# The per-head score loop of a hybrid decoder step: sample memories at steps 1 to 16 instead of 2 to 17

## The reference

```python
def step(carry, inp):
    C, n, m = carry
    qc, kc, vc, ic, fc = inp
    b = jnp.cumsum(fc, axis=-1)
    d = jnp.where(causal, b[..., :, None] - b[..., None, :] + ic[..., None, :], -jnp.inf)
    inter = b + m[..., None]
    m_t = jnp.maximum(inter, jnp.max(d, axis=-1))
    s = jnp.einsum('bhtd,bhsd->bhts', qc, kc) * jnp.exp(d - m_t[..., None])
    a = jnp.exp(inter - m_t)
    num = a[..., None] * jnp.einsum('bhtd,bhdv->bhtv', qc, C) + jnp.einsum('bhts,bhsv->bhtv', s, vc)
    den = a * jnp.einsum('bhtd,bhd->bht', qc, n) + jnp.sum(s, axis=-1)
    h = num / jnp.maximum(jnp.abs(den), jnp.exp(-m_t))[..., None]
    ...
    C_new = decay[..., None, None] * C + jnp.einsum('bhsd,bhsv->bhdv', wk, vc)
```

## Time and profile before

| | |
|---|---|
| median of 3 runs | 3322.55 us |
| the profiled execution | 3323.48 us, of which its span is 3321.7 us |
| PE busy in the span | 95% |
| DVE, ACT, POOL busy | 43%, 24%, 24% |
| score loops: length, from the first product behind the prompt's memory to END's numerators | head 0 104.8, head 1 102.9, head 2 103.5, head 3 103.5 us |

### The profile page before, as it was taken

One profiled execution on the slowest core, in us unless ns is written; L12 is line 12 of the kernel. 1 busy time (PEld: TensorE's weight loads), 2 busy tenths in 40 slices (PEclk: granted clock), 3 DMA queues, 4 the chain that ended last, 5 costly groups with the idle time before them and its releaser, 6 DMA issues.

```text
span 3321.7 us, 51916 instructions
## 1 busy us (share of the span) xinstructions
PE 3161.0 (95%) x20960; PEld 2913.0 (88%) x20960; DVE 1437.7 (43%) x2086; ACT 810.3 (24%) x1525; POOL 813.4 (24%) x519
## 2 busy tenths in 40 slices
PE   6999899999999999999888999899899999999997
PEld 5777599999999989999767877777898999999996
DVE  2000435333333354343338595858425433333335
ACT  4111524111111124111234344343104211111113
POOL 2111033333223232333101010101332333333320
PEclk9999899999999999999889999999899999999998
DMA  7544311111111113333335554636511111111111
GB/s 213 136 119 112 97 39 51 51 44 44 38 51 50 38 45 125 113 111 109 121 129 184 176 199 161 214 120 235 203 41 38 51 51 44 48 47 44 44 38 53
DMA packets 275649, 318.07 MB, mean 96 GB/s; under 512 B 23565, under 2 KB 215309, under 8 KB 274298
## 3 DMA queue, kind: packets, MB, share of 16 engines
q1 hardware_dynamic: 255265, 250.27, 24.6%
q10 hardware_dynamic: 12960, 40.04, 3.1%
q0 software_dynamic: 7296, 25.96, 2.3%
HBM read 224.88 MB, written 92.19 MB: 95 GB/s over the span
## 4 chain that ended last, share of the span: by engine, by line
PE 80%; DVE 9%; ACT 5%; issue 3%; DMA 2%; SPq 0%; DVEq 0%; ACTq 0%
PE ps L366 22%; PE ps L367 22%; PE ps L368 22%; PE ps L1852 3%; PE ps L1046 1%; DMA CT<-in_state_mlstm_C 1%; PE ps L1026 1%; ACT X L449 1%; PE ps L1055 1%; DVE CT L1388 1%; PE ps L1056 1%; PE ps L1057 1%; DVE DN L1498 1%; PE ps L387 1%; PE ps L743 1%
## 5 line engine op out<-in xcount | busy, mean ns | idle before, releaser
L366 PE MATMUL ps<-AH,WH 128*128 128x352 f32 x3072 | 1000.7, 326 | 11.2 <-DVE AL L2298 6.2
L367 PE MATMUL ps<-AL,WH 128*128 128x352 f32 x3072 | 986.3, 321 | 0.0
L368 PE MATMUL ps<-AH,WL 128*128 128x352 f32 x3072 | 986.2, 321 | 0.0
L353 POOL TENSOR_SCALAR WH<-RAW 128x1024 fp32r<-128x1024 f32 x200 | 234.6, 1173 | 1734.3 <-PEq L373 1661.8
L366 PEld LDWEIGHTS ps<-AH,WH 128*128 128x128 f32 x3072 | 577.7, 188 | 37.7 <-issue 23.5
L367 PEld LDWEIGHTS ps<-AL,WH 128*128 128x128 f32 x3072 | 579.1, 189 | 1.0
L368 PEld LDWEIGHTS ps<-AH,WL 128*128 128x128 f32 x3072 | 577.4, 188 | 0.0
L355 POOL TENSOR_TENSOR WL<-RAW,WH 128x1024 fp32r<-128x1024 f32 x200 | 507.7, 2538 | 16.7
L366 PE MATMUL ps<-HH,WH 128*128 128x352 f32 x1536 | 498.4, 324 | 0.0
L367 PE MATMUL ps<-HL,WH 128*128 128x352 f32 x1536 | 492.3, 320 | 0.0
L368 PE MATMUL ps<-HH,WL 128*128 128x352 f32 x1536 | 491.9, 320 | 0.0
(11 more groups left out here) (287 smaller groups left out, 3482.8 us busy)
## 6 DMA issues: line engine op xcount, KB each, us to landing
RAW<-in_ffn_w SPq DMA_DIRECT2D x128, 512.0 KB, 3.8
CT<-in_state_mlstm_C SPq DMA_DIRECT2D x32, 1024.0 KB, 8.6
out_C_s<-CT SPq DMA_DIRECT2D x32, 1024.0 KB, 5.5
RAW<-in_ml_w_in SPq DMA_DIRECT2D x32, 512.0 KB, 3.9
RAW<-in_conv_w_pw SPq DMA_DIRECT2D x24, 512.0 KB, 7.5
STK<-u_scratch SPq DMA_DIRECT2D x48, 190.0 KB, 3.5
xc_scratch<-XC ACTq DMA_DIRECT2D x16, 528.0 KB, 2.7
so_scratch<-SO ACTq DMA_DIRECT2D x16, 528.0 KB, 3.7
```

Source lines behind the costliest of these rows:

```text
L353: pool.tensor_scalar(WH[:, k % 4], RAW[:, k % 2], 1.0, 0.0, ALU.mult, ALU.add).then_inc(w_hi, 1)
L366: pe.matmul(ps[:, bank, 0:CW], wh[:, k, cols], hi[:, k, cs], start=(k == 0), stop=False)
L367: pe.matmul(ps[:, bank, 0:CW], wh[:, k, cols], lo[:, k, cs], start=False, stop=False)
L368: mm = pe.matmul(ps[:, bank, 0:CW], wl[:, k, cols], hi[:, k, cs], start=False, stop=(k == nk - 1))
```

## The change

Two numbers change. SLOT0 becomes 1 and LAST[DEC] becomes 16:

```diff
         DEC, END = 3, 4
-        LAST = {0: 1, 1: 5, 2: 11, DEC: 17, END: 19}
-        SLOT0 = 2
+        LAST = {0: 1, 1: 5, 2: 11, DEC: 16, END: 19}
+        SLOT0 = 1
         IS_STEP = SLOT0 + 2 * DEC_B - 2
```

## The result

The changed kernel takes 3327.39 us (median of 12 runs, 3324.85 to 3331.53), the kernel before on the same chip 3321.33 us (12 runs, 3318.05 to 3323.64): +6.1 us, ratio 1.002, 95% interval 1.0013 to 1.0028. The forecast was 3331 us, 8 us above the kernel before. Slower is the right direction, and 3327.39 lies in the forecast's own range, at its lower end, somewhat nearer to rival B's 3325 than to 3331. The change is 0.18%: by the 0.2% that the prediction asked of a measurable change it would still count as none, while the interval leaves out 1.

The account below looks back on a forecast made before the run. Bound: load 7's release, its length, then PE's work to the denominators. Per head -3.45 + 2.0 + 0.6 + 3.4 = +2.55 us, head 0 +0.65; +8.3 on 3322.55 gives 3331 us, own range 3327 to 3335.

Parts of the forecast that it names:

- rival B: No measurable change, 3325 us: clock stays up at sample 5's read, slow stretch behind sums costs no more; chance 0.24.
- term 1: Sample 5's last update on DVE moves from step 13 to 12, releasing load 7 sooner: -3.45 us a head.
- term 2: DVE is later from step 1 on, by late scores of pair 3 and a second update: +2.0 us a head.
- term 3: Sample 5's read, step 11: its load wait may lower the clock and delay pair 13's scores: +0.6 us (0 to 1.2).
- the load itself: Load 7, of the last sample memory, keeps its length of 9.28 us: 0.
- term 4: One more step of prompt work on PE between load 7's landing and the denominators, partly at low clock: +3.4 us.
- its own sign: In the profile after, the prediction counts as wrong if load 7's wait is gone; 1 to 2.3 us was expected.
- Rival A: The clock falls at load 7's read as well, some 2.1 us per head: 3339 us; chance 0.20.
- Term 5: ACT's copy of the old sums gives DVE pair 18's weights 0.5 us later, hidden by a cover of 4.6 us.
- Head 0: Special case: the wait for load 4 goes, worth -1.9 us, so its loop changes by +0.65 us.

Follow-up runs that it names:

- e9: e6 with DVE's six copies and splits of the tokens moved ahead of its first weighting: 3325.3 us.
- e11: e5 with DVE's six copies and splits of the tokens moved ahead of its first weighting: 3319.9 us.
- e8: The changed kernel with five filler matmuls (results unused) on PE ahead of sample 5's read: 3324.8 us.
- e1: The kernel before, with SP issuing the load of sample b+2 ahead of its wait for sample b's last update: 3326.4 us.
- e2: The changed kernel, with SP issuing the load of sample b+2 ahead of its wait for sample b's last update: 3325.6 us.
- e10: e6 with the sample sums and the denominators' place put back by one step: 3320.8 us.
- e12: e6 with both edits, token splits first as in e9 and sample sums one step later as in e10: 3322.3 us.
- e6: e2 plus filler matmuls (6 and 6, results unused) ahead of PE's two long waits for numerators: 3324.5 us.
- e5: e1 plus filler matmuls (5 and 6, results unused) ahead of PE's two long waits for numerators: 3317.0 us.
- e7: The kernel before with five filler matmuls (results unused) on PE ahead of sample 5's read: 3316.7 us.

## Why the prediction was right, and where not

Head by head the sum can be followed with the measured terms, all counted from the loop's start, as differences to the kernel before. The first three rows give the fourth, by how much load 7 is issued later; the fourth to the seventh give the last:

| | predicted | head 1 | head 2 | head 3 |
|---|---|---|---|---|
| term 1, one step sooner | -3.45 | -3.45 | -3.45 | -3.45 |
| term 2, start (delay at pair 12) | +2.0 | +2.15 | +2.14 | +2.14 |
| term 3, load 5 (further delay at pair 13) | +0.6 | +1.57 | +3.64 | +0.22 |
| load 7's issue, as measured | -0.85 | +0.29 | +2.34 | -1.08 |
| from there to sample 7's read ("the load itself") | 0 | -1.64 | -1.59 | -1.62 |
| term 4, from the read to the denominators | +3.4 | +3.67 | +4.55 | +3.34 |
| from the denominators to END's numerators | 0 | -0.08 | -0.47 | +0.90 |
| loop | +2.55 | +2.24 | +4.83 | +1.54 |

The first three rows add up to the fourth within 0.02 us in every head. Term 1 is the old spacing, kept as it was predicted.

**Term 2 was right in size**: +2.15 for +2.0, and 1.41 for the 1.35 that the scores of pair 3 come later. Its reason was half right. The wait for the mask is there (1.21 us; 1.5 predicted), but e9 and e11 show the same 1.4 us without it: the read and the quarter ahead of the scores are enough.

**Term 3 is the step that was mis-sized**: 0.2 to 3.6 us, mean 1.8 over three heads, where 0.6 with ends of 0 and 1.2 stood. The waits of 1.70 and 2.12 us that it took as a guide were for load 4; those for load 5 were 0, 2.01, 1.25 and 1.85 us in heads 0 to 3. Two more numbers were missing. The load takes 10.5 to 10.8 us instead of 9.6 to 9.8, perhaps since its issue moved closer to POOL's two transfers of 512 KB. And the low clock, when it comes, can take the whole of the scores (3.62 us). e8 takes the wait away and gives heads 1 and 2 back 1.4 and 3.4 us.

**The load itself was put at 0 and gave 1.6 us a head.** The prediction kept load 7 at 9.28 us. In heads 1 to 3 it takes 7.1 to 7.4 us, and PE reaches the read 7.68 us behind the issue instead of 9.3. No reason for the shorter load was found. With it the bound that the forecast named, landing of load 7 plus PE's work, is gone: PE's read comes 0.2 to 0.6 us behind the landing. The prediction had called itself wrong if load 7's wait was gone, and in three of four heads it is; by its own sign its mechanism failed there. Load 7 is not far from binding, though: e8 waits for it in every head. e1 and e2 show that the wait is not what keeps the loops long either: without any wait for loads they stay at 104.7 to 105.8 us. Rival A, the clock falling at load 7's read too, so had no place to happen; its mechanism was real, but at load 5.

**Term 4 was near**: +3.7, +4.6 and +3.3 for +3.4. The order costs, as e10 and e12 show (3.7 and 3.0 us over four heads). The share of the clock in it was too small: the scores of pair 19 took 1.96 us at the low clock, 0.9 more than at the full one, where 0.4 was put for the whole slow stretch.

**A wait that the prediction does not have** stands behind the denominators in head 3, 1.47 us for the store of tile 2. It is there in head 3 of every kernel with the samples at slot 1 except e9 (0.24 to 2.12 us), and in none with them at slot 2.

**Term 5**: not quite hidden. DVE gets the weights of pair 18 some 0.5 us later, as predicted (it waits 2.25 for 1.77 us), but in heads 1 to 3 PE waits 0.35 us for ACT's copy of the old sums, to which ACT comes only behind the gain (until 1988.55 in the chain). The prediction looked at DVE's wait there and not at PE's.

**Head 0**: the wait for load 4 is gone, as predicted, which is worth 1.5 us by pair 12 where 1.9 was put. Sample 5's read waits 2.01 us and the clock stays up, so term 3 is nothing there; from the read of sample 7 to the denominators it is +2.5 instead of +3.4. The loop is 0.5 us shorter where +0.65 stood.

So the total of +8.1 for +8.3 in the loops is right partly by luck. In heads 1 to 3 term 3 was too small by 1.2 us on average and term 4 by 0.45, and the 1.6 us by which PE's read follows sooner on load 7's issue made up for them. The measured time is also 2 us under the loops' sum, by differences outside them that nobody predicted. The direction was not luck: the start (2 us a head at pair 12) and the end's order each cost, as e6, e10 and e5 show with the loads out of the way.

## What to carry to other kernels

When two engines take turns as the bound, taking a wait away moves the idle time instead of removing it; look where it gathers, because one piece of idle on PE can bring the low clock and cost more than several short ones. Where an idle piece can't go, a few matmuls in it may pay: 11 in each head made e1 into e5, 9 us faster. Look at more than one pass of a loop before naming the cause, too: e7 was faster in heads where its reason did not apply. And before moving work one step sooner, write down what each of its transfers will then run beside, and what stands behind it on the engine that is slowest at that moment.

## What the runs showed of the hardware

The length of a wait does not by itself tell whether the clock falls. In the kernel before, 2.01 us at sample 5's read in head 1 were followed by a clock of 0.50. In the changed kernel the same 2.01 us in head 0 were not, nor were 2.74 us in head 2 of e2. Timeline of PE and the window behind it:

```profile
1795.71 1.06 PE L1114 MATMUL ps<-CT,QZ 128*32 128x512 f32 x8 [2.01 <-DMA CT<-in_state_mlstm_C]
```
```profile
1797.00:1799.00 2.00, 2.00 (x11) 1.71 (x10) 1.97 (x4) 0.00 (x0) 0.36 (x1) 1.00 1.01 291
```

Loops with the same instructions in one execution so differ by 3.2 us (head 2 against heads 1 and 3), and single heads shouldn't be compared without looking at their clock.

The clock also falls with PE recorded as busy: in e10 the windows at the sample sums show PE busy for all of their 2.00 us when it goes from 1.00 to 0.50, and in e6 the only wait near is one of 0.35 us ahead of the sums. What runs there are the 32-column products of the sums, in some 4 us. It is not so in every head: in head 0 of e7 the clock stays at 1.00 through them. None of the runs changed these products, so that they are the cause is argued and not shown; e10 gained by putting less work behind them. How long the low clock lasts behind them differs from head to head (0.57 to 1.00 over the same 8 us in e7), and the loops differ with it.
